# Two norms, the Fourier mixer and the order of the held rests, in a fused two-network kernel

## Chip, cores and metric

One core of one Trainium2 chip. The metric is device time in microseconds of one execution (us), the median of the runs. The engines are TensorE (PE, its weight loads PEld), VectorE (DVE), ScalarE (ACT), GpSimd (POOL) and SyncE (SP), which issues most loads.

## What is computed

Two networks one after the other on 256 tokens of 1024 features. The first has two layers on two streams (the tokens and a context of 256, together 512 columns); the layer's mixer is a two-dimensional Fourier transform in layer 0 and a retention in layer 1:

```python
def _rmsnorm(h, g):
    y = h32 * lax.rsqrt(jnp.mean(h32 * h32, axis=-1, keepdims=True) + NORM_EPS)
    return (y * g.astype(jnp.float32)).astype(h.dtype)
def _modnorm(h, g, shift, scale):
    return _rmsnorm(h, g) * (1.0 + scale) + shift
def _fourier_mixer(u, w_out):        # u = _modnorm(h, ...), per stream
    ug = u.astype(jnp.float32).reshape(b, n, FFT_GROUPS, FFT_GROUP_W)
    f = jnp.real(jnp.fft.fft2(ug, axes=(1, 3), norm='ortho'))
    return f.reshape(b, n, d).astype(u.dtype) @ w_out
# first_block, per layer: feed-forward half, mixer, feed-forward half
    return _rmsnorm(h, final_norm_g)
```

The retention projects the tokens (256) to q, k, v and g and the context (256) to k and v. The second network (two layers) takes the result of that final norm, begins each layer with an rmsnorm and a wide projection, and ends each with a mixture of 16384 experts (128 blocks of 128), of which the first 24 blocks' hidden values are computed early and held.

## The kernel before

Activations lie with features on the partitions: 8 tiles (KD) of 128 features by 256 (N) or 512 (2N) token columns. Every weight product is made of three float32r products (lines 254 to 256, `product`): rounded weight with rounded input, with the input's rest, and the weight's rest with the rounded input. Weights come as blocks of 1 MB into a ring of four (RING). ScalarE rounds each half block into one of two slots (`round`, line 242), GpSimd takes the rest (`leave_rest`, line 270) once that half is rounded. A stage is a class with one method per engine; each engine runs the stages' methods in order, and `stage_done` counts stages. `lead` is called by a stage to round the next stage's first two blocks (ROUNDED).

`Norm` (class at line 579): ScalarE squares 8 tiles (line 638), TensorE sums them (671, 676), ScalarE and VectorE make the reciprocal root (643, 696), TensorE spreads it to PSUM (680); then VectorE scales each tile (716). With `parts`, ScalarE adds the shift and rounds (658) and VectorE takes the rest (706), two tiles behind; without, ScalarE adds the shift in place. The order of tiles is features outer, streams inner. If the stage before is a `Project` or `PeerExperts`, squares start as each tile of x is ready (`early`, line 622).

`Fourier` (line 950), between the second norm of layer 0 and a `Project`: for each of 16 tiles (8 groups, 2 streams) TensorE turns the 256 tokens in two halves of 128 with a 128 x 256 table of cosines and sines (982) into a PSUM bank, ScalarE copies 512 columns (1013), TensorE multiplies with the tables along tokens, four products (992, 994), ScalarE rounds (1022), VectorE takes the rest (1030). All are plain fp32. `half(0)`, then `self.next.lead(act)` (1016), then the loop over tiles. Before the loop ScalarE issues the store of a bias table (`start.store`).

`Retention` (1051): TensorE's `columns_of` makes 4 query blocks on 256 columns and 4 key blocks on 512; in the first, `input_tile` waits for both streams of a feature tile.

The final norm of the first network writes to a separate place, and `Replace` (its copy is line 3330) brings it back to x; the next norm follows.

`PeerExperts` (3072 on): a loop over 104 blocks, then 12 pairs of held blocks. For each half e of a pair VectorE weighs (3281), ScalarE rounds (3221) and VectorE takes the rest (3283) of the activation, TensorE adds 12 products (3145), and ScalarE rounds a half of the next pair's weights (3234): of pair n+1 only the second half after pair 0, then both halves of n+2, and so on. GpSimd goes through the halves as in the loop: first half of j, second half of j - 1.

Of the kernel before, what the change touches and what calls it, by code (L numbers as in the profile page):

```python
# [578 lines left out]
class Norm(Stage):  # L579
# [7 lines left out]
    def __init__(self, chip, out, sq, small, tokens, bank, mod=None, gain=None, parts=None, kept=None, tables=None, mods=None,  # L587
                 lead=None, slots=(4, 5, 6)):
# [31 lines left out]
    def act(self, act, link):  # L620
        c, nc = self.chip, self.nc
        early = isinstance(self.before, (Project, PeerExperts))
# [29 lines left out]
        if self.parts or self.mod is not None:  # L652
# [8 lines left out]
            if not self.parts:  # L661
                last.then_inc(self.chip.stage_done, 1)
# [25 lines left out]
    def dve(self, dve, link):  # L688
# [32 lines left out]
        if self.parts:  # L721
            for i in range(len(self.tiles) - lag, len(self.tiles)):
                rest_of(i)
            dve.wait_ge(self.input_split.sem, self.input_split.at(len(self.tiles)))
            dve.sem_inc(c.stage_done, 1)
        elif self.mod is None:
            dve.wait_ge(self.scaled.sem, self.scaled.at(len(self.tiles)))
            dve.sem_inc(self.chip.stage_done, 1)
# [7 lines left out]
def first_norm(chip, tokens, mod, mods, split=True, lead=None):  # L736
# [3 lines left out]
                tokens, 7, mod=mod, parts=first_input(chip, tokens) if split else None, mods=mods, lead=lead)  # L740
# [209 lines left out]
class Fourier(Stage):  # L950
# [3 lines left out]
    def __init__(self, chip, start):  # L954
        super().__init__(chip)
        self.start = start
        cst = chip.at(A_CST1, NCST1)
        self.dft = cst[:, 0:256]
        self.cosn = cst[:, 256:768].rearrange("p (t n) -> p t n", t=NT)
        self.sinn = cst[:, 768:1280].rearrange("p (t n) -> p t n", t=NT)  # L960
        self.u = chip.at(A_U, KD, 2 * N)
        self.half = chip.at(A_WORK, 4, NT, 2 * P)
        a_f = A_WORK + 4 * NT * 2 * P
        self.parts = tuple(chip.parts_at(a_f + i * KD * 2 * N, KD, 2 * N) for i in range(2))
        n = 2 * KD
        self.by_feature = chip.signals("dft_by_feature", n)
        self.half_ready = chip.signals("dft_half_ready", n)
        self.by_token = chip.signals("dft_by_token", n)
        self.rounded = chip.signals("rounded", n)
        self.kept = chip.signals("dft_kept", n)  # L970

    def pe(self, pe):
        pe.wait_ge(self.chip.stage_done, self.index)
        pe.wait_ge(self.chip.cst1_loaded, 16)
        ps, n = self.chip.ps, 2 * KD

        def along_features(i):
            s, g = divmod(i, KD)
            if i >= 4:
                pe.wait_ge(self.half_ready.sem, self.half_ready.at(i - 3))  # L980
            for t in range(NT):
                last = self.nc.tensor.matmul(ps[:, i % 4, t * 256:(t + 1) * 256],
                                             self.u[:, g, s * N + t * P:s * N + (t + 1) * P], self.dft,
                                             start=True, stop=True)
            last.then_inc(self.by_feature.sem, 1)

        def along_tokens(i):
            pe.wait_ge(self.half_ready.sem, self.half_ready.at(i + 1))
            if i >= 4:
                pe.wait_ge(self.kept.sem, self.kept.at(i - 3))  # L990
            for t in range(NT):
                self.nc.tensor.matmul(ps[:, 4 + i % 4, 0:N], self.half[:, i % 4, t, 0:P], self.cosn[:, t, :],
                                      start=t == 0, stop=False)
                last = self.nc.tensor.matmul(ps[:, 4 + i % 4, 0:N], self.half[:, i % 4, t, P:2 * P], self.sinn[:, t, :],
                                             start=False, stop=t == NT - 1)
            last.then_inc(self.by_token.sem, 1)

        along_features(0)
        for i in range(n):
            if i + 1 < n:  # L1000
                along_features(i + 1)
            along_tokens(i)

    def act(self, act, link):
# [3 lines left out]

        def half(i):
# [3 lines left out]
            copy(self.half[:, i % 4].rearrange("p t c -> p (t c)"), ps[:, i % 4, :], ACT.Copy).then_inc(self.half_ready.sem, 1)  # L1013

        half(0)
        self.next.lead(act)
        for i in range(2 * KD):
            if i + 1 < 2 * KD:
                half(i + 1)
            s, g = divmod(i, KD)  # L1020
            act.wait_ge(self.by_token.sem, self.by_token.at(i + 1))
            copy(self.parts[0][:, g, s * N:(s + 1) * N], ps[:, 4 + i % 4, 0:N], ACT.Copy).then_inc(self.rounded.sem, 1)

    def dve(self, dve, link):
        dve.wait_ge(self.chip.stage_done, self.index)
        for i in range(2 * KD):
            s, g = divmod(i, KD)
            cols = slice(s * N, (s + 1) * N)
            dve.wait_ge(self.rounded.sem, self.rounded.at(i + 1))
            last = self.nc.vector.tensor_tensor(self.parts[1][:, g, cols], self.chip.ps[:, 4 + i % 4, 0:N],  # L1030
                                                self.parts[0].bitcast(F32)[:, g, cols], ALU.subtract)
            last.then_inc(self.kept.sem, 1)
        dve.wait_ge(self.kept.sem, self.kept.at(2 * KD))
        dve.sem_inc(self.chip.stage_done, 1)

# [15 lines left out]
class Retention(Stage):  # L1051
# [73 lines left out]
    def pe(self, pe):  # L1125
        nc, ps = self.nc, self.chip.ps

        def columns_of(j, out, tokens):

            whi, wlo = self.weights(j)  # L1130
            for e in range(2):
                pe.wait_ge(self.chip.rest_done[e], self.split_count(j))
                for k in range(KD):
                    i = e * KD + k
                    if j == 0 and e == 0:
                        self.input_tile(pe, k)
# [4 lines left out]
        for j in range(4):  # L1141
            columns_of(j, lambda e: ps[:, j, e * N:(e + 1) * N], N)
        pe.wait_ge(self.chip.cst1_loaded, 32)
# [1928 lines left out]
class PeerExperts(Stage):  # L3072
# [164 lines left out]
    def pool(self, pool, link):  # L3237
# [429 lines left out]
```

## Time and profile before

| | |
|---|---|
| runs of the kernel | 4455.31 to 4460.98 us, median 4459.0 (3 runs) |
| profiled execution | 4452.6 us, its span 4450.8 |
| busy, share of span | PE 96%, PEld 82%, POOL 58%, DVE 42%, ACT 42% |
| mean granted clock of TensorE | 0.986 |

The span is the time from the first to the last instruction of one profiled execution. Busy shares are averages over stages with different limits; a matmul's end is modelled.

### The profile page before, as it was taken

Reading aid. Unit: us, or ns where it says so; the run is one execution under the profiler, and the core shown is the slowest. Engines: PE = TensorE matmul, PEld = TensorE weight load, DVE = VectorE, ACT = ScalarE, POOL = GpSimd, SP = SyncE. Lnnn points to the kernel's source line nnn. Section 1 sums busy time; section 2 is a strip of 40 time slices with the busy share of each in tenths; the row PEclk is TensorE's granted clock in tenths of the full one; section 3 lists DMA queues with packets and bytes.
Section 4 is the critical chain, followed back from the end, with each engine's and each line's share of the span. In section 5 each row is a group of like instructions: output and inputs, shape, how many; then the busy total and the mean of one; then the engine's idle time right before and its main releaser. Section 6 shows DMA issues by size and latency. Waiting matters only on the chain.

```text
span 4450.8 us, 62594 instructions
## 1 busy us (share of the span) xinstructions
PE 4260.6 (96%) x24214; PEld 3659.1 (82%) x24214; DVE 1881.2 (42%) x3564; ACT 1851.2 (42%) x3014; POOL 2594.8 (58%) x1262
## 2 busy tenths in 40 slices
PE   7999999999999999889999999999989999999998
PEld 5877787878878899877899888887877998888886
DVE  5751377032022332454568322223565488222224
ACT  4433343232233444443333555554451434555554
POOL 3443244444444378631367888887730568888886
PEclk9999999999999999999999999999999999999999
DMA  7643367222222244441143355555530342555554
GB/s 264 218 163 91 90 232 268 100 88 102 95 104 95 77 160 182 174 161 39 67 166 119 142 187 186 186 186 206 175 142 29 112 168 72 189 189 186 186 186 159
DMA packets 110658, 661.37 MB, mean 149 GB/s; under 512 B 11632, under 2 KB 18032, under 8 KB 41200
## 3 DMA queue, kind: packets, MB, share of 16 engines
q1 hardware_dynamic: 99648, 638.27, 40.7%
q10 hardware_dynamic: 10800, 20.15, 1.7%
q8 instruction: 150, 2.46, 0.2%
q14 instruction: 60, 0.49, 0.0%
HBM read 647.89 MB, written 10.49 MB: 148 GB/s over the span
## 4 chain that ended last, share of the span: by engine, by line
PE 81%; DVE 11%; ACT 3%; POOL 2%; DMA 1%; issue 1%; SPq 0%; ACTq 0%; DVEq 0%; POOLq 0%
PE ps L3145 15%; PE ps L254 13%; PE ps L255 13%; PE ps L256 13%; PE ps L3135 9%; PE ps L3136 4%; PE ps L1665 2%; PE ps L3049 2%; POOL ring_rest L270 2%; DVE arena L2521 1%; PE ps L2837 1%; ACT rounded L242 1%; PE ps L2190 1%; DVE arena L3024 1%; PE ps L2208 1%
## 5 line engine op out<-in xcount | busy, mean ns | idle before, releaser
L270 POOL TENSOR_TENSOR ring_rest<-ring,rounded 128x1024 fp32r<-128x1024 f32 x940 | 2299.7, 2461 | 1318.4 <-ACT rounded L242 1117.3
L254 PE MATMUL ps<-part,rounded 128*128 128x512 f32 (+1 forms) x3360 | 1148.1, 342 | 34.4 <-DVE part L706 21.5
L255 PE MATMUL ps<-part,rounded 128*128 128x512 f32 (+1 forms) x3360 | 1140.0, 339 | 0.0
L256 PE MATMUL ps<-part,ring_rest 128*128 128x512 f32 (+1 forms) x3360 | 1139.5, 339 | 0.0
L242 ACT ACTIVATE rounded<-ring 128x1024 fp32r<-128x1024 f32 x484 | 485.5, 1050 | 645.8 <-PE ps L256 638.0
L254 PEld LDWEIGHTS ps<-part,rounded 128*128 128x128 f32 x3360 | 644.1, 192 | 120.3 <-DVE part L706 21.7
L256 PEld LDWEIGHTS ps<-part,ring_rest 128*128 128x128 f32 x3360 | 644.2, 192 | 67.3
L255 PEld LDWEIGHTS ps<-part,rounded 128*128 128x128 f32 x3360 | 644.5, 192 | 66.7
L3234 ACT ACTIVATE rounded<-ring 128x1024 fp32r<-128x1024 f32 x456 | 481.7, 1056 | 317.4 <-DMA ring<-in_weights 315.4
L3145 PE MATMUL ps<-rounded,part 128*128 128x512 f32 x2048 | 593.8, 394 | 18.3 <-POOL ring_rest L270 13.4
L3135 PE MATMUL ps<-x_parts,rounded 128*128 128x512 f32 x1664 | 594.0, 397 | 1.5 <-ACTq L3069 1.5
L3136 PE MATMUL ps<-x_parts,ring_rest 128*128 128x256 f32 x1664 | 466.7, 280 | 0.0
L3145 PEld LDWEIGHTS ps<-rounded,part 128*128 128x128 f32 x2048 | 371.1, 189 | 102.3 <-POOL ring_rest L270 18.1
L3135 PEld LDWEIGHTS ps<-x_parts,rounded 128*128 128x128 f32 x1664 | 312.6, 188 | 76.6 <-ACTq L3069 1.8
L3265 DVE TENSOR_TENSOR ps<-ps,arena 128x256 f32<-128x256 f32 x208 | 129.9, 624 | 523.2 <-ACT ps L3202 523.2
L3145 PE MATMUL ps<-ring_rest,part 128*128 128x512 f32 x1024 | 321.5, 395 | 0.0
L3136 PEld LDWEIGHTS ps<-x_parts,ring_rest 128*128 128x128 f32 x1664 | 313.8, 189 | 8.0
L444 DVE SCALAR_TENSOR_TENSOR ps<-arena,ps 128x512 f32<-128x512 f32 x392 | 269.4, 747 | 10.2 <-DMA arena<-in_mod_weights 7.8
L3145 PEld LDWEIGHTS ps<-ring_rest,part 128*128 128x128 f32 x1024 | 192.7, 188 | 47.3
L933 DVE SCALAR_TENSOR_TENSOR x<-ps,mods,x 128x256 f32<-128x256 f32 x80 | 35.8, 480 | 456.2 <-PE ps L256 456.2
L822 ACT ACTIVATE arena<-ps 128x512 f32<-128x512 f32 (+1 forms) x88 | 47.9, 544 | 401.2 <-PE ps L256 401.2
L1665 PE MATMUL ps<-arena,ring 128*128 128x256 f32 x704 | 179.7, 396 | 12.5 <-DMA ring<-in_weights 11.0
(372 smaller groups left out, 5219.6 us busy)
## 6 DMA issues: line engine op xcount, KB each, us to landing
ring<-in_weights SPq DMA_DIRECT2D x528, 1024.0 KB, 4.8
arena<-in_mod_weights SPq DMA_DIRECT2D x128, 512.0 KB, 4.3
arena<-in_mod_lead SPq DMA_DIRECT2D x8, 1024.0 KB, 18.1
held<-arena ACTq DMA_DIRECT2D x24, 256.0 KB, 5.5
arena<-held SPq DMA_DIRECT2D x24, 256.0 KB, 4.7
arena<-bias_scratch ACTq DMA_DIRECT2D x2, 2048.0 KB, 8.6
bias_scratch<-arena ACTq DMA_DIRECT2D x1, 3072.0 KB, 32.5
x<-in_x SPq DMA_DIRECT2D x1, 2048.0 KB, 10.1
```

What stands on the lines that cost most here:

```text
L242: self.nc.scalar.activation(c.rounded[:, s % ROUNDED, half], c.ring[:, slot, half], ACT.Copy)\
L254: mm(out, w[0], a[0], start=start, stop=False)
L255: mm(out, w[0], a[1], start=False, stop=False)
L256: return mm(out, w[1], a[0], start=False, stop=stop)
L270: eng.tensor_tensor(c.ring_rest[:, slot, half], c.ring[:, slot, half], c.rounded[:, (self.s0 + r) % ROUNDED, half].bitcast(F32), ALU.subtr ...
L444: v.scalar_tensor_tensor(bank, self.chunk_row(i, k), self.cond[:, k, stream:stream + 1], bank, ALU.mult, ALU.add)\
L1665: last = self.nc.tensor.matmul(c.ps[:, self.BANK, e * N:(e + 1) * N], c.ring[:, slot, i, :], self.whole[:, k, :], start=k == 0, stop=k == ...
L3135: nc.tensor.matmul(c.ps[:, r % 2, :], whi[:, k, :], c.x_parts[:, k, :], start=k == 0, stop=False)
L3136: last = nc.tensor.matmul(c.ps[:, r % 2, 0:N], wlo[:, k, :], self.z[0][:, k, :], start=False, stop=k == KD - 1)
L3145: last = nc.tensor.matmul(self.out(t, i), a, w[:, i * 4 * P:(i + 1) * 4 * P], start=False, stop=end and n == 2)
L3234: self.nc.scalar.activation(c.rounded[:, (self.s0 + r) % ROUNDED, half], c.ring[:, f % RING, half], ACT.Copy)\
L3265: v.tensor_tensor(gelu, gelu, self.gates[:, :, bass.ds(b + HELD, 1)].rearrange("p t a -> p (t a)"), ALU.mult)\
```

## The change

Four edits:

1. `Norm` gets `by_stream`: the norm ahead of the retention takes all 8 tiles of the tokens, then those of the context. TensorE's query blocks 0 and 1 are begun tile by tile, both blocks' first halves together, with a wait for each token tile; blocks 2 and 3 follow; a wait for the last tile stands before the key blocks.
2. The final norm of the first network scales x in place, `Replace` is gone, and the norm behind it squares each tile as soon as it is scaled (`early` takes `Norm` too).
3. In the held tail GpSimd takes the rests in the order in which ScalarE rounds.
4. The norm ahead of `Fourier` makes statistics only (`statistics`, no tiles). `Fourier` scales, adds the shift, and folds: since cosine is even and sine odd in the token index, 256 tokens become 128 sums and 128 differences of token k and token 256 - k, with token 0 apart in a tile `first` that is zero but for its first column. Along features there are now 3 products of 128 columns, along tokens 2 of 256; the tables in `constants` are cut and scaled to fit. Loops are staggered: VectorE scales tile i, folds i - 2, takes the rest of i - 6; ScalarE adds the shift of i, copies i - 2, rounds i - 4, and rounds a half of the next stage's weights in iterations 6, 8, 10 and 12. PSUM banks for the results are three, where there were four.

```diff
@@ Norm
-        self.tiles = [(d, s) for d in range(KD) for s in range(tokens // N)]
+        self.tiles = [] if statistics else [(d, s) for d in range(KD) for s in range(tokens // N)]
+        if by_stream:
+            self.tiles = [(d, s) for s in range(tokens // N) for d in range(KD)]
         self.scaled = chip.signals("scaled", len(self.tiles))
+        self.x_ready = self.scaled
...
-        early = isinstance(self.before, (Project, PeerExperts))
+        early = isinstance(self.before, (Project, PeerExperts, Norm))
@@ Fourier, pe
+            pe.wait_ge(self.folded.sem, self.folded.at(i + 1))
             if i >= 4:
                 pe.wait_ge(self.half_ready.sem, self.half_ready.at(i - 3))
...
+            mm(ps[:, i % 4, 0:P], self.even[:, i % 4, :], self.cos_f, start=True, stop=True)
+            mm(ps[:, i % 4, P:2 * P], self.odd[:, i % 4, :], self.sin_f, start=True, stop=False)
+            mm(ps[:, i % 4, P:2 * P], self.first[:, i % 4, :], self.cos_f, start=False, stop=True)\
+                .then_inc(self.by_feature.sem, 1)
...
+            if i >= self.OUT_BANKS:
+                pe.wait_ge(self.kept.sem, self.kept.at(i - self.OUT_BANKS + 1))
+            mm(ps[:, self.bank(i), 0:N], self.half[:, i % 4, 0:P], self.cos_t, start=True, stop=False)
+            mm(ps[:, self.bank(i), 0:N], self.half[:, i % 4, P:2 * P], self.sin_t, start=False, stop=True)\
+                .then_inc(self.by_token.sem, 1)
@@ Fourier, act
-        half(0)
-        self.next.lead(act)
...
+        for i in range(self.n + self.KEPT_BEHIND):
+            if i < self.n:
+                bias(i)
+            if 0 <= i - self.HALVED_BEHIND < self.n:
+                half(i - self.HALVED_BEHIND)
+            if i >= self.KEPT_BEHIND:
+                keep(i - self.KEPT_BEHIND)
+            if 6 <= i < 14 and i % 2 == 0:
+                j, h = divmod(i // 2 - 3, 2)
+                self.next.round(act, j, halves=(h,))
+        self.next.led = ROUNDED
@@ Fourier, dve
+        v.memset(self.first, 0.0).then_inc(self.cleared.sem, 1)
...
+            first = s * N
+            near, far = self.u[:, g, first + P:first:-1], self.u[:, g, first + P:first + 2 * P]
...
+            v.tensor_copy(self.first[:, i % 4, 0:1], self.u[:, g, first:first + 1])
+            v.tensor_tensor(self.even[:, i % 4, :], near, far, ALU.add)
+            v.tensor_tensor(self.odd[:, i % 4, :], near, far, ALU.subtract).then_inc(self.folded.sem, 1)
...
+        for i in range(self.n + self.SCALED_AHEAD):
+            if i < self.n:
+                scale(i)
+            if 0 <= i - self.FOLDED_BEHIND < self.n:
+                fold(i - self.FOLDED_BEHIND)
+            if i >= self.SCALED_AHEAD:
+                rest(i - self.SCALED_AHEAD)
@@ Retention, pe
+        for k in range(KD):
+            pe.wait_ge(split.sem, split.at(k + 1))
+            for j in range(2):
+                if k == 0:
+                    pe.wait_ge(self.chip.rest_done[0], self.split_count(j))
+                of_query(j, 0, k)
+        for j in range(2):
+            pe.wait_ge(self.chip.rest_done[1], self.split_count(j))
+            for k in range(KD):
+                last = of_query(j, 1, k)
+            last.then_inc(self.chip.block_done, 1)
+        for j in range(2, 4):
             columns_of(j, lambda e: ps[:, j, e * N:(e + 1) * N], N)
+        pe.wait_ge(split.sem, split.at(2 * KD))
@@ PeerExperts, pool
-        for j in range(n, self.blocks):
+        for j in (n, n + 1):
             self.leave_rest(j, 0, self.split_count(j))
             self.leave_rest(j - 1, 1, self.split_count(j - 1))
-        self.leave_rest(self.blocks - 1, 1, self.split_count(self.blocks - 1))
+        for j in range(n + 1, self.blocks):
+            self.leave_rest(j, 1, self.split_count(j))
+            if j + 1 < self.blocks:
+                self.leave_rest(j + 1, 0, self.split_count(j + 1))
@@ second_network
-    stages = [second_norm(chip, columns(vec, "final_g")), Replace(chip)]
+    small = [chip.at(B_SMALL + i * N, N) for i in range(2)]
+    stages = [Norm(chip, chip.x[:, :, 0:N], chip.at(B_SQ, KD, N), small, N, 5, gain=columns(vec, "final_g"))]
```

## Rows read from the trace of the kernel before

**Rows 1.** The page, chain that ended last, shares by engine

```profile
PE 81%; DVE 11%; ACT 3%; POOL 2%; DMA 1%; issue 1%; SPq 0%; ACTq 0%; DVEq 0%; POOLq 0%
```

**Rows 2.** Chain in order of time, 395 to 490: start us, us, what

```profile
421.21 6.50 ACT arena L658 x16
427.75 2.09 PE ps L982 x4
430.36 3.88 ACT rounded L242 x4
...
436.78 0.86 PE ps L982 x4
...
473.17 0.50 PE ps L254
```

**Rows 3.** Windows: stretch, its us, busy of five engines, granted clock, DMA share, GB/s

```profile
422.00:423.00 1.00, 0.00 (x0) 0.00 (x0) 1.00 (x3) 1.00 (x4) 0.00 (x0) 0.51 0.00 0
...
432.00:433.00 1.00, 1.00 (x5) 0.83 (x5) 0.00 (x0) 1.00 (x2) 1.00 (x1) 0.87 0.88 100
```

**Rows 4.** Timeline of TensorE, 2051.5 to 2053.5: start, us, engine, line, form, count

```profile
2052.16 0.39 PE L2207 MATMUL ps<-arena 128*128 128x128 f32 x2
2052.38 0.39 PE L2208 MATMUL ps<-arena 128*128 128x128 f32 x2
```

**Rows 5.** Timelines of VectorE at 420 and 2372; group of L1030 (busy us, mean ns)

```profile
420.70 6.35 DVE L716 SCALAR_TENSOR_TENSOR arena<-x,mods,ps 128x256 f32<-128x256 f32 x16 [1.25 <-PE ps L680]
2372.85 0.42 DVE L2979 TENSOR_TENSOR arena<-arena 128x256 f32<-128x256 f32 x1
...
L1030 DVE TENSOR_TENSOR part<-ps,part 128x256 fp32r<-128x256 f32 x16 | 6.8, 425 | 39.2 <-ACT part L1022 39.2
```

**Rows 6.** L3281 by source (ns min/median/max); timelines of VectorE and GpSimd, 4404 to 4440

```profile
L3281 DVE TENSOR_TENSOR ps<-arena x48: 624/826/2825, 3049.2 to 4426.6; 128x256 f32<-128x256 f32 x48
...
4417.55 2.83 DVE L3281 TENSOR_TENSOR ps<-arena 128x256 f32<-128x256 f32 x1
4415.17 4.73 POOL L270 TENSOR_TENSOR ring_rest<-ring,rounded 128x1024 fp32r<-128x1024 f32 x2 [2.23 <-ACT rounded L3234]
```

**Rows 7.** Retention's start: chain in order of time; timeline of ScalarE

```profile
1278.86 0.40 DVE part L706
...
1291.97 0.34 ACTq L1258 DMA_DIRECT2D arena<-in_expo  x1
1297.22 2.01 ACT L242 ACTIVATE rounded<-ring 128x1024 fp32r<-128x1024 f32 x2 [6.00 <-PE ps L256]
...
1302.98 2.01 ACT L242 ACTIVATE rounded<-ring 128x1024 fp32r<-128x1024 f32 x2 [3.27 <-PE ps L256]
```

**Rows 8.** Final norm: timelines of ScalarE and VectorE, 1806 to 1845

```profile
1811.12 1.99 ACT L242 ACTIVATE rounded<-ring 128x1024 fp32r<-128x1024 f32 x2
1818.02 2.56 ACT L638 ACTIVATE arena<-x 128x256 f32<-128x256 f32 x8 [4.90 <-DVE x L3330]
...
1812.13 3.22 DVE L716 SCALAR_TENSOR_TENSOR arena<-x,vec,ps 128x256 f32<-128x256 f32 x8 [0.80 <-PE ps L680]
1815.51 2.47 DVE L3330 COPY x<-arena 128x2048 f32<-128x2048 f32 x1 [0.16 <-DVEq L728]
...
1821.76 0.43 DVE L694 COPY arena<-ps 128x256 f32<-128x256 f32 x1 [3.78 <-PE ps L671]
```

**Rows 9.** Held tails: timelines of GpSimd and ScalarE; waits of both (us in total, times, longest)

```profile
3058.25 5.13 POOL L270 TENSOR_TENSOR ring_rest<-ring,rounded 128x1024 fp32r<-128x1024 f32 x2 [5.68 <-ACT rounded L3234]
...
3070.72 5.13 POOL L270 TENSOR_TENSOR ring_rest<-ring,rounded 128x1024 fp32r<-128x1024 f32 x2 [2.24 <-ACT rounded L3234]
...
3056.84 0.39 ACT L3221 ACTIVATE part<-ps 128x256 fp32r<-128x256 f32 x1 [1.41 <-PE ps L3145]
...
3059.56 0.39 ACT L3221 ACTIVATE part<-ps 128x256 fp32r<-128x256 f32 x1 [1.39 <-PE ps L3145]
...
PE ps L3145 <- POOL ring_rest L270: 6.3, 5, 1.3
...
PE ps L3145 <- POOL ring_rest L270: 7.2, 6, 1.3
```

More of the change, by code:

```diff
@@ L660, in act @@
                     last.then_inc(self.rounded.sem, 1)
-            if not self.parts:
+            if self.tiles and not self.parts:
                 last.then_inc(self.chip.stage_done, 1)
@@ L725, in dve @@
             dve.sem_inc(c.stage_done, 1)
+        elif not self.tiles:
+            dve.sem_inc(c.stage_done, 1)
         elif self.mod is None:
@@ L961, in __init__ @@
         self.u = chip.at(A_U, KD, 2 * N)
-        self.half = chip.at(A_WORK, 4, NT, 2 * P)
-        a_f = A_WORK + 4 * NT * 2 * P
+        self.even, self.odd, self.first = (chip.at(A_SQ + i * 4 * P, 4, P) for i in range(3))
+        self.half = chip.at(A_WORK, 4, 2 * P)
+        a_f = A_WORK + 4 * 2 * P
         self.parts = tuple(chip.parts_at(a_f + i * KD * 2 * N, KD, 2 * N) for i in range(2))
-        n = 2 * KD
-        self.by_feature = chip.signals("dft_by_feature", n)
-        self.half_ready = chip.signals("dft_half_ready", n)
@@ L972, in pe, with tile, bank @@
+        self.by_token = chip.signals("dft_by_token", self.n)
+        self.rounded = chip.signals("rounded", self.n)
+        self.kept = chip.signals("dft_kept", self.n)
+    def tile(self, i):
+        s, g = divmod(i, KD)
+        return s, g, slice(s * N, (s + 1) * N)
+    def bank(self, i):
+        return 4 + i % self.OUT_BANKS
     def pe(self, pe):
-        pe.wait_ge(self.chip.stage_done, self.index)
         pe.wait_ge(self.chip.cst1_loaded, 16)
-        ps, n = self.chip.ps, 2 * KD
+        ps, mm = self.chip.ps, self.nc.tensor.matmul
@@ L977, in along_features @@
         def along_features(i):
-            s, g = divmod(i, KD)
+            s, g, cols = self.tile(i)
+            pe.wait_ge(self.folded.sem, self.folded.at(i + 1))
             if i >= 4:
                 pe.wait_ge(self.half_ready.sem, self.half_ready.at(i - 3))
[L981 to L984, printed above, removed]
@@ L991, in along_tokens @@
[L991 to L996, printed above, removed]
+            if i >= self.OUT_BANKS:
+                pe.wait_ge(self.kept.sem, self.kept.at(i - self.OUT_BANKS + 1))
@@ L1007, in act, with bias @@
         self.start.store(act)
+        def bias(i):
+            s, g, cols = self.tile(i)
+            act.wait_ge(self.scaled.sem, self.scaled.at(i + 1))
+            copy(self.u[:, g, cols], self.u[:, g, cols], ACT.Identity, bias=self.mods[:, 3, g, s:s + 1]).then_inc(self.biased.sem, 1)
         def half(i):
@@ L1024, in dve @@
-    def dve(self, dve, link):
[L1025 to L1028, printed above, removed]
-            dve.wait_ge(self.rounded.sem, self.rounded.at(i + 1))
[L1030 to L1033, printed above, removed]
+            copy(self.half[:, i % 4, :], ps[:, i % 4, 0:2 * P], ACT.Copy).then_inc(self.half_ready.sem, 1)
@@ new lines, in keep @@
+        def keep(i):
+            s, g, cols = self.tile(i)
+            act.wait_ge(self.by_token.sem, self.by_token.at(i + 1))
+            copy(self.parts[0][:, g, cols], ps[:, self.bank(i), 0:N], ACT.Copy).then_inc(self.rounded.sem, 1)
+        for i in range(self.n + self.KEPT_BEHIND):
[8 more added lines that the diff above has]
+                self.next.round(act, j, halves=(h,))
@@ L1139, in columns_of, with of_query @@
             last.then_inc(self.chip.block_done, 1)
-        for j in range(4):
+        split = self.before.input_split
+        def of_query(j, e, k):
+            w, i = self.weights(j), e * KD + k
+            return self.product(ps[:, j, e * N:(e + 1) * N], [x[:, i, :] for x in w], [x[:, k, 0:N] for x in self.u],
+                                k == 0, k == KD - 1)
+        for k in range(KD):
[10 more added lines that the diff above has]
+        for j in range(2, 4):
             columns_of(j, lambda e: ps[:, j, e * N:(e + 1) * N], N)
+        pe.wait_ge(split.sem, split.at(2 * KD))
         pe.wait_ge(self.chip.cst1_loaded, 32)
@@ L3415, in first_network @@
                                table=dft if first else None)
-        stages.append(first_norm(chip, 2 * N, 1, mods, split=layer > 0))
+        stages.append(first_norm(chip, 2 * N, 1, mods, split=layer > 0, by_stream=layer > 0, statistics=layer == 0))
         if layer == 0:
-            fourier = Fourier(chip, start)
+            fourier = Fourier(chip, start, mods)
             stages += [fourier, Project(chip, tiles_of(fourier.parts), KD, 2 * N, gate=5, mods=mods)]
```

68 lines of the change are left out of this document (39 added, 29 removed).

## The prediction, written before the changed kernel was run

> **What bounds the kernel now.** I read the page first: TensorE is busy 96% of the span and holds 81% of the chain that ended last [rows 1]. So an edit pays only where that chain leaves TensorE, or where TensorE's own work shrinks. Then I read the chain, the waits and the timelines of the four places that the diff touches. Times below are us from the span's start.
>
> Fourier: the norm's rstd is ready at 420.70. Then 16 scalings and 16 biases run to 427.7 with TensorE idle, TensorE makes its first products at half clock [rows 2, 3], ScalarE rounds four weight halves in one block to 434.2 while TensorE waits for the second copied tile, and from 434.8 TensorE is the limit until the next stage's first matmul at 473.17 [rows 2]. The stage is 52.5 long.
> Retention: tiles alternate between the two token halves; the first is ready at 1278.86 + 0.40 = 1279.3, the last just before 1291.97, 0.84 each, and TensorE puts its 3 products only on pairs. Blocks of 48 products then end 5.76 apart (1297.22, 1302.98: 0.12 a product), the fourth at 1302.98 + 2 × 5.76 = 1314.5 [rows 7].
> Final norm: scaling, a copy of 2.48, then squares that wait for it [rows 8].
> Held tail: every second pair TensorE waits for two rests in a row on GpSimd: 12.47 from one to the next, where its own work is 4 × 2.72 = 10.88 (ScalarE's copies follow the ends of its 12-product halves) [rows 9].
>
> **Fourier.** Removed per tile: 6 fp32 products of 256 columns at 0.43 (x4 stands for two, 0.86) = 2.59 [rows 2]. Added: 3 of 128 columns and 2 of 256. A 128-column product, two instructions, takes 2052.38 − 2052.16 = 0.22 [rows 4]. So 3 × 0.22 + 2 × 0.43 = 1.53 per tile, 24.5 for 16.
> VectorE per tile: scaling 0.40 (16 in 6.35); add and subtract 128 wide, bounded by 0.42 for 256 wide with both inputs in SBUF and by half of it, I take 0.22 each, since starts overlap; copy of one column, between nothing and that 0.21, I take 0.13; rest 0.42; estimated 0.06 of waits: 1.45 [rows 5]. ScalarE per tile: bias 0.41 (16 in 6.50) and two copies of the same width, 1.2; the four weight roundings (3.88) now lie in iterations 6 to 12, 1.45 on average [rows 2]. So three engines lie within 0.1 of each other, TensorE last. The first of them that slips sets the end.
> Start: memset (512 wide, under two of 0.42 [rows 5], I take 0.6 with the stage's handshake), scaling, bias, two further scalings ahead in the queue, fold: 0.6 + 1.2 + 0.65 after 420.70, so the first matmul at 423.3 where it was 427.75. The clock fell to its lower level, 1.2 GHz, at 422 and came back to 2.4 after 432, 4.4 after TensorE began again [rows 3]; it would fall here too and cost about 2.2. Then 423.3 + 24.5 + 2.2 = 450.0, plus the last rounding copy and rest 0.9 = 450.9.
> Moved: the four roundings are now made while VectorE is busy, so GpSimd's four rests (2.4 each) fall among the folds. In the held tail VectorE's product of two SBUF operands takes 0.62 at least and 2.83 at most; that longest one ended at 4420.38, 0.48 after GpSimd's two rests (4415.17 + 4.73) [rows 6]; a fold has two SBUF operands twice per tile, while scaling and rest have one and PSUM. VectorE does some 0.8 of other work before it comes to the next fold, so up to 2.4 − 0.8 = 1.6 is lost per rest, 6.4 for four, of which the 0.2 per tile by which ScalarE's roundings already slow the loop hide about 2: I add 4, bounds 0 and 9.6. End at 455; bounds 448.7 (clock stays, no loss) and 463. Gain 473.2 − 455 = **18**, between 10 and 24.
> The Trainium skill's page SBUF — State Buffer (section Who interferes with whom) says that a VectorE instruction with two SBUF inputs and a GpSimd instruction that reads SBUF lock each other out for a whole instruction. By that rule the folds must wait, as the row shows; without it the stage's end would be 451 and the gain 22.
> Hidden: the bias table's store keeps its place (0.33 of ScalarE's queue, ahead of the first bias, under VectorE's memset and scaling). The next stage's weights are rounded by 446, before they are asked for.
>
> **Retention.** From 1279.3 on TensorE puts 6 products on each tile of the first half. At half clock that is 6 × 0.24 = 1.4 > 0.84, so it stays busy and the clock should return some 4.4 later (1283.7, 18 products done); the other 78 of the first two blocks take 78 × 0.12 = 9.4 and end at 1293.1. What is late next: the third block's rest. Its rounding stands behind ScalarE's norm tiles and a table's DMA (to 1291.97 + 0.34), then 1.0 and 2.4 on GpSimd: TensorE waits until 1295.9. From there GpSimd (4.8 per block) and TensorE (5.76) run as before: 1295.9 + 2 × 5.76 = 1307.4. Gain 1314.5 − 1307.4 = 7.1. The wait of 2.8 may drop the clock again (up to 1.7): I take **6.5**, between 3.5 and 8 [rows 7]. The key products come long after 1291.97, so TensorE's new wait for the last tile is free.
>
> **Final norm.** Gone: the copy of 2.48. New overlap: squares follow the scalings tile by tile, but ScalarE still has 1.99 of rounding to 1813.1, so eight squares at 0.32 end at 1815.8 where they ended at 1820.6, and the sums reach VectorE at 1816.3 instead of 1821.76: **5.4**, between 4 and 7 (the idle stretch of TensorE gets shorter, which can only help its clock) [rows 8].
>
> **Held tail.** ScalarE rounds first the second half of the second pair, then both halves of the third, and so on; GpSimd takes rests in another order, so the ready one stands behind one that waits for a rounding. In the new order both agree. The rest (p+1, second half) can then start when products (p−1, second half) end + 0.4 + 1.0, and is asked for three halves (8.2) later: 3.8 of work in 8.2. The idle time shown is 6.3 in one layer and 7.2 in the other [rows 9]; a stall shown as 1.26 costs 12.47 − 10.88 = 1.59, as a matmul's modelled end hides a part, so 13.5 × 1.59 / 1.26 = 17.0. Given back: VectorE's SBUF product adds to GpSimd's time where they meet (5.13 for two rests at 3058.25, 4.73 at 4415.17), some 2.75 per half against TensorE's 2.72, just balanced; I take off 2: **15**, between 10 and 17. Weights come one block per 5.44 instead of 6.2; the waits of the tail name no DMA [rows 9].
>
> **Sum.** 18 + 6.5 + 5.4 + 15 = 45. Span 4450.8 → 4406; the profiled execution was 4452.6 (1.8 around the span), so 4407.8. The median of the runs is 6.4 above the profiled one, 4459.0, so I predict 4459 − 45 = **4414**. Nothing between the places is bound by an absolute time: weights are fetched four blocks behind the blocks done, so what is saved moves all that follows.
>
> **Rivals.**
> A. The folds hardly meet GpSimd (VectorE has slack, or takes its turn first): Fourier gains 22 to 24: 4409. For it: the small overlap needed; against it: the long product of [rows 6]. 0.17.
> B. Fourier stays at the lower clock: TensorE waits a little for each fold, copy and bank. Per tile 3.06 instead of 1.53: the gain of 18 becomes 473.2 − (423.3 + 49 + 0.9) = 0: 4432. For it: the clock fell soon after TensorE stopped here; against it: at that rate TensorE would be busy throughout, and such a stretch brought the clock back [rows 3]. [...] 0.08.
> C. The held tail does not get what it should: GpSimd and VectorE's SBUF product (2.40 + 0.49 = 2.89 if they never overlap, over 2.72) take the place of the order, 24 × 0.17 = 4 per layer, or the order was not the cause: gain 8 or less: 4421 to 4429. 0.14.
> D. Slower: the folds read one operand backwards along the tokens, which no row here shows. 32 such instructions; beyond the 0.22 each, they undo all 45 at 1.4 each, and make the kernel slower by over 0.2% (8.9) from 1.7 each, about 1.9 for 128 elements; at 2.2 each the time is 4459 − 45 + 32 × 2 = 4478. Nothing speaks for such a price but that it is unseen. 0.02.
> E. Two or more of B, C, a slow fold, and a lost retention gain together leave under 9: 0.02.
> My forecast, 4405 to 4424: 0.57.
>
> The range: up to B's 4432, down to all gains at their upper bounds (24 + 8 + 7 + 17 = 56: 4403, less 3 for the spread of the runs): 4400 to 4432. About 0.2% (8.9) is what this kernel's measurement can tell from no change: faster 0.96, same 0.02, slower 0.02.
>
> **What would show it.** Fourier: first matmul near 423, the Project stage's first near 455, copies and folds of 2 to 3 where a rest of GpSimd runs, and the clock at full speed from 428. Retention: query blocks' last product near 1307 (less what came before), one wait of about 3 for the third block's rest. Final norm: squares start within 1.5 of the first scaling, no copy line. Held tail: no TensorE wait for GpSimd after the first pair, 65 instead of 76 to 78 per layer. Wrong would be: folds over 0.4 with GpSimd idle; ScalarE as the stage's limit with waits for PSUM banks (three instead of four); stalls in the tail that name VectorE.

## The result, and the profile after

The changed kernel was measured three times, each time beside the kernel before; the ratio and its 95% interval are estimated from the runs of both.

| | median (us) | before beside it | difference of medians | ratio, 95% interval |
|---|---|---|---|---|
| changed, first | 4410.35 (4408.89 to 4418.05) | 4459.99 | 49.6 | 0.9898 [0.9886, 0.9909] |
| changed, second | 4416.95 (4414.73 to 4420.52) | 4461.12 | 44.2 | 0.9901 [0.9885, 0.9918] |
| changed, third | 4413.52 (4409.95 to 4419.35) | 4460.81 | 47.3 | 0.9898 [0.9881, 0.9914] |

Predicted were 4414 and a gain of 45. The profiled execution of the first took 4411.17, its span 4409.4, against 4452.6 and 4450.8: 41.4 less. Executions of one kernel beside each other lie 2 to 11 us apart in most cases, 16 and 19 in two, and the intervals reach 5 to 8 us to either side, so whole times decide little below that; the places of the four edits are read in the traces. "Trace after" is the first one.

The page of the changed kernel, the chain by engine (to set beside [rows 1]) and TensorE's products of the expert stage, before and after (the last figures are its idle time ahead of them, in all, and what ended most of it):

```profile
PE 82%; DVE 11%; ACT 3%; DMA 1%; issue 1%; POOL 1%; SPq 0%; ACTq 0%; DVEq 0%; POOLq 0%
...
L3145 PE MATMUL ps<-rounded,part 128*128 128x512 f32 x2048 | 593.8, 394 | 18.3 <-POOL ring_rest L270 13.4
...
L3216 PE MATMUL ps<-rounded,part 128*128 128x512 f32 x2048 | 591.1, 394 | 4.9 <-DVE part L3342 4.9
```

GpSimd is gone from what ended the idle time of these products; the 4.9 are two waits at the start of the two tails (a tail is the stretch of the held blocks).

**Fourier.** The trace after, timeline of its start, with start, duration, engine, line, operation and idle time before it (these answer to the first of [rows 2]):

```profile
419.26 0.48 DVE L1055 MEMSET arena<- 128x512 f32 x1 [1.51 <-DVEq L730]
420.71 0.15 DVE L1071 COPY arena<-arena 128x1 f32<-128x1 f32 x1
420.78 0.28 DVE L1072 TENSOR_TENSOR arena<-arena 128x128 f32<-128x128 f32 x1
420.98 0.29 DVE L1073 TENSOR_TENSOR arena<-arena 128x128 f32<-128x128 f32 x1
421.18 0.48 DVE L1059 SCALAR_TENSOR_TENSOR arena<-x,mods,ps 128x256 f32<-128x256 f32 x1
421.41 0.55 PE L1000 MATMUL ps<-arena 128*128 128x128 f32 x1 [2.45 <-DVE arena L1073]
```

What VectorE pays is the time from one start to the next: 0.07 for the one-column copy, 0.20 each for the sum and the difference. No cost of reading one operand backwards is seen: 0.28 for 128 columns, where 256 columns read forwards take 0.42 [rows 5]. Each of GpSimd's four rests holds up one fold. Two of these folds, the two rests that they meet, and all four waits of TensorE, from the same trace (the L1010 rows show where a tile's last product starts):

```profile
432.55 2.09 DVE L1072 TENSOR_TENSOR arena<-arena 128x128 f32<-128x128 f32 x1
435.55 2.15 DVE L1072 TENSOR_TENSOR arena<-arena 128x128 f32<-128x128 f32 x1
...
432.13 2.36 POOL L270 TENSOR_TENSOR ring_rest<-ring,rounded 128x1024 fp32r<-128x1024 f32 x1 [35.24 <-ACT rounded L242]
435.19 2.35 POOL L270 TENSOR_TENSOR ring_rest<-ring,rounded 128x1024 fp32r<-128x1024 f32 x1 [0.71 <-ACT rounded L242]
...
433.75 0.60 PE L1010 MATMUL ps<-arena 128*128 128x256 f32 x2
434.89 0.49 PE L1000 MATMUL ps<-arena 128*128 128x128 f32 x2 [0.55 <-DVE arena L1073]
...
436.10 0.59 PE L1010 MATMUL ps<-arena 128*128 128x256 f32 x2
437.95 0.49 PE L1000 MATMUL ps<-arena 128*128 128x128 f32 x2 [1.26 <-DVE arena L1073]
...
439.16 0.60 PE L1010 MATMUL ps<-arena 128*128 128x256 f32 x2
...
443.36 0.49 PE L1000 MATMUL ps<-arena 128*128 128x128 f32 x2 [0.55 <-DVE arena L1073]
446.43 0.49 PE L1000 MATMUL ps<-arena 128*128 128x128 f32 x2 [1.26 <-DVE arena L1073]
```

A fold of 2.09 ends at 434.64, 0.15 after the rest that began at 432.13 (434.49). A tile takes TensorE 1.53 where nothing waits; from 433.75 to 436.10 it took 2.35, and from there to 439.16 it took 3.06. So the two waits cost 0.82 and 1.53, and the same pair comes once more: 4.7 in all. From the spread's end (418.96) to Project's first product (454.68) the stage is 35.7 long where it was 52.5.

**Retention.** The wait for the third block's rest, trace after, and the clock around it (columns of the windows: stretch, length, TensorE's busy time with its count of products, granted clock, share of the DMA engines, GB/s):

```profile
1280.31 0.39 PE L254 MATMUL ps<-part,rounded 128*128 128x256 f32 x1 [3.45 <-POOL ring_rest L270]
```

```profile
1261.90:1263.70 1.80, 0.05 (x2) 0.96 0.00 0
1263.70:1267.00 3.30, 3.30 (x16) 0.51 0.00 0
1267.00:1276.80 9.80, 9.80 (x83) 1.00 0.17 51
1276.80:1280.30 3.50, 0.06 (x1) 1.00 1.01 421
1280.30:1284.00 3.70, 3.69 (x18) 0.54 0.76 321
1284.00:1290.00 6.00, 6.00 (x52) 1.00 0.18 35
```

The clock falls to its lower level, 1.2 GHz, twice, each time behind a pause. The fourth query block is copied 33.63 after the first scaling instead of 38.82.

**Final norm.** Trace after, ScalarE and VectorE (to set beside [rows 8]): the eight squares stand right behind ScalarE's rounding, under the scalings, and the second norm's first scaling is 6.84 behind the first one's, where it was 12.02.

```profile
1789.81 3.22 DVE L719 SCALAR_TENSOR_TENSOR x<-x,vec,ps 128x256 f32<-128x256 f32 x8 [0.80 <-PE ps L683]
1788.80 1.99 ACT L242 ACTIVATE rounded<-ring 128x1024 fp32r<-128x1024 f32 x2
1790.69 2.79 ACT L641 ACTIVATE arena<-x 128x256 f32<-128x256 f32 x8
...
1796.65 1.27 DVE L719 SCALAR_TENSOR_TENSOR ps<-x,vec,ps 128x256 f32<-128x256 f32 x3 [0.80 <-PE ps L683]
```

**Held tail.** GpSimd in layer 1's tail (to set beside [rows 9]), and two of VectorE's products of two SBUF operands:

```profile
3029.47 2.41 POOL L270 TENSOR_TENSOR ring_rest<-ring,rounded 128x1024 fp32r<-128x1024 f32 x1 [0.34 <-ACT rounded L3305]
3040.35 2.55 POOL L270 TENSOR_TENSOR ring_rest<-ring,rounded 128x1024 fp32r<-128x1024 f32 x1 [0.21 <-ACT rounded L3305]
3043.07 41.04 POOL L270 TENSOR_TENSOR ring_rest<-ring,rounded 128x1024 fp32r<-128x1024 f32 x15 [0.17 <-ACT rounded L3305]
...
3026.08 0.62 DVE L3355 TENSOR_TENSOR ps<-arena 128x256 f32<-128x256 f32 x1
3083.22 1.38 DVE L3355 TENSOR_TENSOR ps<-arena 128x256 f32<-128x256 f32 x1
```

GpSimd first idles 0.34 ahead of a rest, and then makes 15 in a row at 41.04 / 15 = 2.74, while TensorE needs 2.72 a half and never waits behind the tail's first product. Rests and VectorE's products both get longer as the tail goes on; it ends before that costs anything.

**The account.** From place to place the two traces give: Fourier 16.8, retention 5.2, final norm 5.2, tails 7.9 and 9.0: 44.1. The span shrank by 41.4. The 2.7 between lie where no edit is: 1.7 gained before Fourier, 2.8 lost between Fourier and the retention, 1.5 and 1.3 gained in the two stretches between retention, final norm and first tail, 4.2 lost between the tails (the remaining 0.2 is rounding and the kernel's end).

### The profile page after: what moved, and what is told of

Read it like the earlier page. It is cut to its first block, busy times and chain, and to the rows that moved or that the text cites. A ratio compares the mean times of both kernels' runs of the same rounds, so it can differ in the third digit from the quotient of the medians.

```text
span 4409.4 us, 62606 instructions
## 1 busy us (share of the span) xinstructions
PE 4242.5 (96%) x24182; PEld 3649.9 (83%) x24182; DVE 1900.2 (43%) x3612; ACT 1844.9 (42%) x3014; POOL 2598.9 (59%) x1262
## 4 chain that ended last, share of the span: by engine, by line
PE 82%; DVE 11%; ACT 3%; DMA 1%; issue 1%; POOL 1%; SPq 0%; ACTq 0%; DVEq 0%; POOLq 0%
PE ps L3216 16%; PE ps L254 13%; PE ps L256 13%; PE ps L255 13%; PE ps L3206 9%; PE ps L3207 4%; PE ps L1736 2%; PE ps L3120 2%; DVE arena L2592 1%; PE ps L2908 1%; ACT rounded L242 1%; PE ps L2261 1%; POOL ring_rest L270 1%; DVE arena L3095 1%; PE ps L2279 1%
```

## The experiments

**Each edit undone.** Four kernels, each the changed one with one part as before. The edit of the last one, cut from its diff:

```
-        for j in (n, n + 1):
...
+        for j in range(n, self.blocks):
             self.leave_rest(j, 0, self.split_count(j))
             self.leave_rest(j - 1, 1, self.split_count(j - 1))
-        for j in range(n + 1, self.blocks):
...
```

> The changed kernel with the Fourier stage, its tables and the norm ahead of it as before; the other three edits stay. Theory (the saving is made in the stage, but some of it is given back in the stage that computes modulation rows beside the next feed-forward, where TensorE waits for transfers of the modulation weights: 3.89 in the trace after against 2.36 before, and 1.2 for the clock behind it): the kernel is 14 us slower than the changed one (16.8 less 2.8), so 31 to 32 faster than before (0.993), and its trace shows the wait near 2.4. Rival (the longer wait is chance of the transfers and has nothing to do with the saving): it is 17 slower than the changed one, 28 to 29 faster than before (0.9936), and the wait is anywhere between 2.3 and 4.

> The changed kernel with the order of tiles and TensorE's order in the retention as before. Theory (what the two traces show at this place, 5.2 from the first scaling to the end of the fourth query block, is worth the same in the whole time): 5 us slower than the changed kernel, 40 faster than before (0.991). Rival (the wait of 3.45 for the third block's rest and the second fall of the clock are followed by a shorter wait elsewhere, or the 1.5 gained behind 1293 belong to it): 6.5 to 7, so 38 to 39 faster than before.

> The changed kernel with the final norm of network one written to another place and copied back. Theory (only the copy and the squares' start matter): 5.2 us slower than the changed kernel, 40 faster than before (0.991). Rival (the shorter idle stretch also keeps TensorE's clock, which had to come back in the blocks behind it: 1.3 more): 6.5 slower, 39 faster than before.

> The changed kernel with GpSimd's old order of rests in the held tail. Theory (the order made all the waits of the tail): 17 us slower than the changed kernel (7.9 and 9.0), 28 faster than before (0.9937), and TensorE waits for GpSimd again every second pair, about 1.26 each time. Rival (the tail's waits hung on the phase in which the loop ended, which the other edits could have moved): less than 10 slower, without the regular waits.

The kernel before took 4466.62 beside these four (4460.08 to 4470.81). The changed kernel was not measured beside them, so the last column is 47, the mean gain of its three measurements, less the gain that is left.

| undone | median | ratio, 95% interval | below before | length of its place, edit undone / edit in | worth by the whole time |
|---|---|---|---|---|---|
| Fourier | 4433.27 | 0.9929 [0.9916, 0.9943] | 33.4 | 52.51 / 34.3 to 35.9 | 13.6 |
| retention | 4422.44 | 0.9907 [0.9891, 0.9922] | 44.2 | 38.76 / 32.2 to 33.7 | 2.8 |
| final norm | 4428.24 | 0.9921 [0.9907, 0.9934] | 38.4 | 12.05 / 6.8 to 7.0 | 8.6 |
| held order | 4435.22 | 0.9933 [0.992, 0.9947] | 31.4 | 77.65 and 76.06 / 69.85 each | 15.6 |

In sum 40.6 against 47, each with about 6 of uncertainty: the edits add up as far as this can be seen, and the split between retention and final norm is told by the traces, not by whole times. Against the expectations: the theories wanted 31 to 32, 40, 40 and 28 below before, and 33.4, 44.2, 38.4 and 31.4 came; with gains this uncertain the whole time decides none of the first three rivals, and the fourth is out by the waits themselves. With the old order GpSimd's waits are back, five in layer 1's tail, as in [rows 9]; the second tail's 76.06 ran at a clock of 1.00, where the tails of 69.85 lose 1.6 to a stretch at the lower clock (one of a later trace, without it, took 68.26). Set beside each other at one clock (77.65 with 69.85, 76.06 with 68.26), the order is worth 7.8 a layer.

```profile
3037.01 0.73 PE L3216 MATMUL ps<-rounded,part 128*128 128x512 f32 x2 [1.26 <-POOL ring_rest L270]
3049.44 0.73 PE L3216 MATMUL ps<-rounded,part 128*128 128x512 f32 x2 [1.25 <-POOL ring_rest L270]
```

The lost 2.8 behind Fourier: TensorE waits there, in the stage that computes modulation rows beside the next feed-forward half, for sums that need the modulation weights. Of the following rows the first is of the trace after, the second of the kernel with the final norm undone, the third of the one with the held order undone; all three have the same Fourier stage.

```profile
726.88 1.24 PE L503 MATMUL ps<-arena 128*32 128x512 f32 x8 [3.89 <-ACT arena L465]
```

```profile
726.72 1.06 PE L503 MATMUL ps<-arena 128*32 128x512 f32 x8 [1.79 <-ACT arena L465]
```

```profile
727.98 1.07 PE L503 MATMUL ps<-arena 128*32 128x512 f32 x8 [2.30 <-ACT arena L465]
```

Before it was 2.36, with Fourier undone 2.38, with retention undone 3.86. With Fourier undone both marks of that run's theory came (2.38, and a worth of 13.6), but nearly the whole range is seen with one and the same stage ahead of the wait. So it varies from execution to execution, VectorE (2.83 in the trace after) and ScalarE waiting there for transfers of these weights, and the 2.8 is no steady loss; a few tenths given back by Fourier can't be excluded.

**Do the folds wait for GpSimd's instruction, and how long?** First the changed kernel again, to be set beside the kernels that follow.

> The changed kernel itself, on the chip of the kernels beside it, so that they can be set against it. Theory (each edit is worth what its place shows, and the places add up): 44 to 46 faster than before (0.990), with a wait for the modulation weights anywhere from 1.8 to 3.9 that is chance of the transfers. Rival (the whole time is worth less than the places show): above 0.991.

Its stage is 34.60 long with the same four waits (0.55, 1.26, 0.55, 1.25), its wait for the modulation weights 2.76. Then, with the rests of Project's first two blocks cut up:

```
+        if isinstance(self.before, Fourier) and r < ROUNDED:
+            for i in range(h * HALF, (h + 1) * HALF):
+                last = eng.tensor_tensor(c.ring_rest[:, slot, i, :], c.ring[:, slot, i, :],
+                                         c.rounded[:, (self.s0 + r) % ROUNDED, i, :].bitcast(F32), ALU.subtract)
+            last.then_inc(c.rest_done[h], 1)
+            return
```

> The changed kernel, where GpSimd takes the rests of the next stage's first two blocks (those that fall among the folds) in eight instructions of 128 columns each instead of one of 1024. Theory (VectorE's fold, with two operands in SBUF, waits for the end of the GpSimd instruction that runs): a fold waits for one piece only, so no fold of 2.1 is left, the longest is under 0.7, TensorE's four waits of 0.55 and 1.26 (3.6 together) go or fall under 0.3 each, and the kernel is 3 us faster than the changed one. Rival 1 (the fold waits because ScalarE's rounding of the weights delays the shift ahead of it): the waits of TensorE stay. Rival 2 (pieces cost GpSimd so much more that the next stage waits for the last rest): the wait moves to the Project stage's start, nothing is gained.

Median 4408.09 (4404.53 to 4412.11) against 4416.95 (4414.73 to 4420.52), 0.9884 [0.9867, 0.9900] of before. GpSimd's pieces, two of VectorE's slowest folds, and the next wait of TensorE after the stage's first product:

```profile
434.75 14.75 POOL L272 TENSOR_TENSOR ring_rest<-ring,rounded 128x128 fp32r<-128x128 f32 x32 [34.45 <-ACT rounded L242]
...
446.92 0.57 DVE L1078 TENSOR_TENSOR arena<-arena 128x128 f32<-128x128 f32 x1
447.41 0.54 DVE L1079 TENSOR_TENSOR arena<-arena 128x128 f32<-128x128 f32 x1
...
452.62 0.50 PE L254 MATMUL ps<-part,rounded 128*128 128x512 f32 x1 [0.99 <-DVEq L1095]
```

ScalarE's roundings stand where they stood, and all four waits are gone; no fold is over 0.58. So a fold waits for the end of the GpSimd instruction that runs, and rival 1 is out. The Trainium skill's SBUF — State Buffer (Who interferes with whom) says that a VectorE instruction with both inputs in SBUF contends with a GpSimd instruction that reads SBUF; the pieces agree. They cost GpSimd 14.75 instead of 9.4, which nobody waits for. The stage is 29.63 long, 5.0 less than in the trace beside it. The expectation counted on the 3.6 of shown waits; but part of a wait is hidden by the modelled end of the matmul before it, and from start to start the four cost 4.7, as worked out above. So the meeting of folds and rests costs 4.7, more than TensorE's idle time shows, and the other 0.3 of the 5.0 is left to the clock. The whole time fell by 8.9 where 3 were expected; only 5.0 of it lie in this stage.

The same by another place of the roundings (the lines that move two of them into the norm ahead are left out here):

```
-            if 6 <= i < 14 and i % 2 == 0:
-                j, h = divmod(i // 2 - 3, 2)
-                self.next.round(act, j, halves=(h,))
+            if self.n < i <= self.n + 2:
+                self.next.round(act, 1, halves=(i - self.n - 1,))
```

> The changed kernel, but ScalarE rounds the next stage's first block in the norm ahead of Fourier (after its squares and after its root, where it has nothing to do), and the second block behind the last shift, so that few of GpSimd's rests meet a fold. Theory (as for the pieces): folds take 0.28 each but for one or two at the start, TensorE's four waits (3.6) go, the stage is 34 or less from the spread's end to Project's first matmul where it was 35.7, and the kernel is 2 to 4 faster than the changed one. Rival (VectorE's 1.2 a tile and ScalarE's are too near to TensorE's 1.53, so the waits come from somewhere else in the loop): 0 to 1.

Median 4412.9 (4410.18 to 4421.1), 0.9895 [0.9879, 0.9912]; the stage is 31.89 long, the four waits are gone, as expected. The gain is 2.3 less than the pieces bring: Project's first product waits 1.97 instead of 0.99 (the two last roundings, begun at 452.93 and 454.14, now stand among the last tiles' copies), and the lower clock lasted 5.6 behind the first product where it lasted 3.0 with the pieces.

**The third block of the retention.**

```
+                if isinstance(self.next, Retention) and i == 12:
+                    self.next.round(act, ROUNDED)
```

> The changed kernel, but ScalarE rounds the retention's third query block between the 13th and the 14th tile of the norm, as soon as the first block is done (about 1274.1 on the clock of the trace after), instead of behind the last tile. Theory (TensorE's wait of 3.45 and the second fall of its clock come from this rounding's place alone): round to 1275.2, GpSimd to 1277.6, so a wait of 0.7 instead of 3.45, no second fall of the clock, and the fourth block ends 4.5 earlier: 4.5 faster than the changed one. Rival (the clock falls again for another reason, or VectorE's late tiles make the key blocks wait): 2.7 or less.

```profile
1278.95 0.39 PE L254 MATMUL ps<-part,rounded 128*128 128x256 f32 x1 [0.80 <-POOL ring_rest L270]
```

This is its only wait among the query blocks. The fourth block's copy is 29.44 after the first scaling, against 33.63 in the trace after and 32.15 in the two other traces of the changed kernel: 4.2 and 2.7. Both numbers of the expectation occur, and the clock decides which: with a second fall the late rounding costs 1.5 more. The whole time, 4414.7 (4412.45 to 4417.38), 0.9898 [0.9881, 0.9914], is 2.3 below that of the changed kernel beside it, which its scatter can't tell from the theory's 4.5 or from 0; the profiled execution also lost 1.4 in the final norm (8.21 instead of 6.84), with the clock at 0.50 from 1791 on.

**The clock.** Last, products whose results nobody uses in two of TensorE's pauses (the 2.45 ahead of Fourier's first product, and the 1.75 ahead of the retention's first, with a like edit that is not shown), alone and with the two improvements, and those two without them. The longer wait for the third block's rest is not filled.

```
+        for _ in range(5):
+            mm(ps[:, 3, 0:256], self.cos_t[:, 0:P], self.cos_t, start=True, stop=True)
         along_features(0)
```

> The changed kernel once more, on the chip of the three kernels beside it. Theory: 0.990 of before, as in its other two measurements; its four waits among the folds are there again (0.55, 1.26, 0.55, 1.26), the length of the stretches at the lower clock varies by 1 to 3 us from execution to execution. Rival (the waits are chance too): another pattern of waits.

> The changed kernel, with five products more (256 columns, result not used) between the spread of the norm ahead of Fourier and the first folded tile, where TensorE waits 2.45, and seven of 128 columns in the 1.75 ahead of the retention's first product. Theory (the clock falls to its lower level, 1.2 GHz, because TensorE pauses there): TensorE has no pause over 0.9 in these places, the clock stays at 2.4 GHz in both or comes back 2 us sooner, and the kernel is 2 to 5 us faster than the changed one. Rival 1 (the clock falls already because of the short waits in the norm, as in the second trace of the changed kernel, where it fell at 423.2 before the spread's end): it falls all the same, the gain is 0 to 1.5. Rival 2 (the added products end late and push the first fold's product): up to 1 slower.

> The changed kernel with the rests in pieces and the third query block rounded early, both as in the runs before. Theory (the two places are independent): 5 and 3 to 4 at their places, 7 to 9 faster than the changed kernel. Rival (the clock's falls are chance and take up what is saved): 3 to 5.

> The kernel with pieces and the early third block, and the added products of the two waits as well. Theory (with no pause left the clock stays up in Fourier and retention): 2 to 5 faster than without them, 10 to 13 faster than the changed kernel. Rival: the same as without them, within 1.

| | median | ratio, 95% interval |
|---|---|---|
| changed, third | 4413.52 (4409.95 to 4419.35) | 0.9898 [0.9881, 0.9914] |
| added products | 4415.64 (4409.72 to 4419.23) | 0.9898 [0.9882, 0.9915] |
| pieces and third block | 4406.55 (4403.73 to 4410.76) | 0.9879 [0.9862, 0.9895] |
| all three | 4404.6 (4395.16 to 4414.44) | 0.9884 [0.9867, 0.9901] |

The third trace of the changed kernel has the same four waits to 0.01. Windows around Fourier's start with the added products, first in the kernel with them alone (its spread ends at 423.47), then in the one with all three (419.50):

```profile
417.00:419.00 2.00, 2.00 (x16) 1.00 0.56 147
419.00:421.60 2.60, 1.25 (x9) 1.00 0.69 290
421.60:423.40 1.80, 1.73 (x9) 0.61 0.00 0
423.40:425.20 1.80, 1.80 (x6) 0.50 0.33 47
```

```profile
415.80:419.50 3.70, 2.28 (x18) 1.00 0.41 175
419.50:424.00 4.50, 4.30 (x25) 1.00 0.68 81
424.00:428.00 4.00, 4.00 (x29) 1.00 0.90 103
428.00:447.00 19.00, 18.84 (x121) 1.00 0.90 104
```

The same work ahead of the place, once with a fall and once without. In the first, the clock fell while TensorE was busy with the norm's spread, ahead of the pause that the products fill, as rival 1 had it. The short pauses of the norm (0.85 and 0.57) can't be the whole cause, since they stand in both executions. The stage was 33.46 long with the added products alone and 28.33 in the kernel with all three, against 35.71 and 30.98 without them in the same group, but one trace each can't tell this from the clock's chance: 34.34 was seen without them too. The added products alone gained nothing in the whole time, against a theory of 2 to 5. With all three, the best single execution of all (4395.16) was seen, but the same kernel also took 4414.44, so the 2.0 between the medians decides nothing. They are not shown to be worth their place. Pieces and third block together are 7.0 below the changed kernel, at the edge of the 7 to 9 of the theory, and have the lowest ratio of all; the pieces alone (0.9884) can't be told from them by the whole time.

## Why the prediction was right, point by point

**Fourier (18 predicted; 16.8 in the first pair, 16.6 to 18.2 over all seven traces that have the stage unaltered).** The first product stood 2.45 behind the spread. That is what the prediction's terms add up to (0.6 + 1.2 + 0.65); its 423.3 has 2.6. 24.5 for TensorE's work held: where nothing waits (the pieces), 26.2 from first to last product, 1.7 of it for the clock. The term of 4 for the folds that meet GpSimd was 4.7. The clock's term of 2.2 lies between what two traces of the changed kernel show: 421.41 to 453.69 is 32.3, less 24.5 and 4.7 leaves 3.1; 426.60 to 457.75 is 31.2 and leaves 2.0. The bound of 463 for the end has 2.5 too much: 450.9 and 9.6 are 460.5; nothing came near it. That the end came at 454.68 where I had 455 owes 1.7 to the start of the trace, which was earlier for no reason of the change. VectorE was mis-sized in the safe direction: 1.2 a tile where I had 1.45 (from start to start, the copy took 0.07 for 0.13, sum and difference 0.20 for 0.22 each, the rest of the activation 0.34 for 0.42), so "three engines within 0.1" was wrong of VectorE. ScalarE's 1.45 held: with the pieces, two tiles and a rounding take it 2.8 of every 3.07 us. TensorE is the limit, and where no fold waits for GpSimd it never waits for either of them. Rival A (no meeting of folds and GpSimd) is out by the four folds of 2.1, B (clock low throughout) by the clock, which is back at 1.00 from 428 on in the trace after, D (backwards read) by 0.28.

**Retention (6.5; measured 5.2 to 6.7).** The mechanism came as written: one wait for the third block's rest, whose end is 18.36 behind the first scaling where I had 18.3. What differs from trace to trace is how soon the clock lets TensorE reach it: the wait was 3.45 with a second fall of the clock, 2.25 without one in the next trace, 2.8 predicted. The second fall that the prediction allowed for (up to 1.7, a bound that none of its rows shows) cost 1.5 where it came.

**Final norm (5.4; 5.0 to 5.2, and 3.8 in the one execution whose clock fell there).** Right in its parts; the sum reached VectorE at 1794.26, 4.45 behind the first scaling, where I had 4.2.

**Held tail (15; 15.6 by traces at one clock, 16.9 in the first pair, 15.6 by the whole time as well).** The order was the cause, and rival C stayed just outside: GpSimd's 2.74 against 2.72, as estimated. One mark was misread: I wrote 65 a layer, 24 halves of 2.72. The 76 to 78 beside it run over 25 halves (300 products) and a stretch at the lower clock, so the mark should have been 68 to 70; measured 69.85. The gain did not rest on it.

**"Nothing between the places is bound by an absolute time"** holds as far as seen: the 2.8 behind Fourier is a wait for transfers that varies from 1.8 to 3.9 whatever stands ahead. The 4.2 between the tails: 2.7 of it lies in two short stretches in which the kernel before, in its one trace, kept the full clock (1.00 from 3499 to 3508 and from 3768 to 3774) and the changed one did not (0.83 and 0.76, as both kernels in layer 0). For the other 1.5 I name no cause. This is scatter of single executions, about as large as the smallest edit.

**The sum (45; 41.4 between the two profiled spans, 49.6, 44.2 and 47.3 between medians).** The mechanisms of the four places carry it, but that it lies so near is partly luck: in the first pair Fourier and retention gave 1.2 and 1.3 less than predicted and the tails 1.9 more, and the rest of the kernel lost 2.7.

## What to carry to other kernels

A step moved beside another engine's work takes its followers along: count which of their instructions hold each other up, and cut the longer one into pieces if nobody waits for its end. Where queues pass work on in pairs, let every engine keep one order; a stall shown as 1.3 in every second pair was 15.6 of the 47. An edit of 5 us in a kernel of 4400 is judged in the trace at its place, from several executions, since the clock alone moves a place by 1.5.

## What the runs showed of the hardware that I had not expected

A VectorE sum or difference of 128 columns with one operand read backwards takes 0.28, and the next starts 0.20 behind it. The traces have no such instruction of 128 columns with both operands forwards; the one of 256 takes 0.42 [rows 5], so no cost of the backward step is seen. An instruction of one column takes 0.15, but the next one starts 0.07 behind it.

The clock's fall doesn't follow from the last pause alone. A pause of 2.2 in the retention was followed by a fall in one trace (the kernel with the pieces) and by none in three others (the changed kernel's second and third, and the one with the held order undone, 2.23 to 2.29). These are the stretches of the pause and behind it, first with the pieces, then of the changed kernel's second trace:

```profile
1273.00:1275.20 2.20, 0.03 (x1) 0.94 0.82 339
1275.20:1278.30 3.10, 3.06 (x14) 0.50 0.99 378
```

```profile
1281.60:1283.90 2.30, 0.04 (x2) 1.00 0.98 381
1283.90:1290.00 6.10, 6.10 (x51) 1.00 0.69 281
```

What decides between them stays open. A fall cost 1.4 to 3.1 at the places read here.
